# Modulation product of an adaptive-norm layer: where its vector steps ride, and how its partial sums cross the partitions

## The reference, cut to what matters

```
c_act = silu(c)
mod = c_act @ w_ada + b_ada                     # 1024 x 6144
shift1, scale1, gate1, shift2, scale2, gate2 = split(mod, 6)
h = rms_norm(x, g_pre_mix) * (1 + scale1) + shift1
y = token_mixer(h, ...)                         # GLU, convolution, attention
x = x + gate1 * rms_norm(y, g_post_mix)
h = rms_norm(x, g_pre_mlp) * (1 + scale2) + shift2
y = square(relu(h @ w_mlp_in)) @ w_mlp_out
x = x + gate2 * rms_norm(y, g_post_mlp)
```

## Time and profile before

| | before |
|---|---|
| median of 3 runs | 1105.59 us (1102.8 to 1105.71) |
| the profiled execution | span 1101.8 us from the first to the last instruction; no time of its own is listed beside it |
| TensorE busy | 1076.2 us, 98% |
| VectorE busy | 814.3 us, 74% |
| ScalarE busy | 550.6 us, 50% |
| POOL busy | 49.7 us, 5% |
| moved by DMA | 205.85 MB |

### The profile page before, as it was taken

The page is one execution under the profiler, slowest core; times in us unless marked ns, Lnnn a source line. Parts: engine busy times, 40 slices in busy tenths (PEclk is TensorE's granted clock), DMA queues, the critical chain, the costliest instruction groups (busy, mean ns, idle before and its releaser), DMA issues.

```text
span 1101.8 us, 18585 instructions
## 1 busy us (share of the span) xinstructions
PE 1076.2 (98%) x7422; PEld 906.7 (82%) x7422; DVE 814.3 (74%) x1163; ACT 550.6 (50%) x682; POOL 49.7 (5%) x58
## 2 busy tenths in 40 slices
PE   9999999999999998999999999999999999999997
PEld 8888888888778777777788888898967888999996
DVE  5665544538689788788999987999997877555554
ACT  6545543436455545553343556375545665444443
POOL 0000000000000441001111000000000000000000
PEclk9999999999999999999999999999999999999999
DMA  9695556453344321969999954374621553565632
GB/s 317 224 273 190 171 172 227 153 192 115 115 153 139 76 54 54 315 213 326 362 330 357 311 188 153 105 230 132 221 78 39 191 191 115 178 204 163 217 117 112
DMA packets 138413, 205.85 MB, mean 187 GB/s; under 512 B 19608, under 2 KB 95661, under 8 KB 138350
## 3 DMA queue, kind: packets, MB, share of 16 engines
q1 hardware_dynamic: 128996, 177.94, 49.6%
q0 software_dynamic: 6560, 25.19, 6.6%
q10 hardware_dynamic: 2794, 1.84, 0.5%
HBM read 202.33 MB, written 1.57 MB: 185 GB/s over the span
## 4 chain that ended last, share of the span: by engine, by line
PE 79%; DVE 13%; DMA 3%; ACT 3%; issue 2%; SPq 0%; POOL 0%; DVEq 0%; ACTq 0%
PE ps L769 22%; PE ps L771 22%; PE ps L770 22%; DVE wl L2594 3%; PE ps L1243 2%; PE ps L995 2%; DMA raw<-in_ffn_w_up 1%; PE ps L1683 1%; DVE wide L3386 1%; DVE wide L2708 1%; PE ps L846 1%; ACT wh L1806 1%; PE ps L1511 1%; PE ps L1180 1%; PE ps L1665 1%
## 5 line engine op out<-in xcount | busy, mean ns | idle before, releaser
L2594 DVE TENSOR_TENSOR wl<-raw,wh 128x2048 fp32r<-128x2048 f32 (+2 forms) x154 | 345.1, 2246 | 84.8 <-ACT wh L1806 84.5
L769 PE MATMUL ps<-wh,xh 128*128 128x512 f32 (+3 forms) x856 | 335.3, 392 | 4.2 <-DVE wl L2594 1.8
L771 PE MATMUL ps<-wl,xh 128*128 128x512 f32 (+3 forms) x856 | 328.3, 384 | 0.0
L770 PE MATMUL ps<-wh,xl 128*128 128x512 f32 (+3 forms) x856 | 327.8, 383 | 0.0
L1806 ACT ACTIVATE wh<-raw 128x2048 fp32r<-128x2048 f32 (+2 forms) x154 | 286.9, 1878 | 50.0 <-PE ps L771 28.4
L769 PEld LDWEIGHTS ps<-wh,xh 128*128 128x128 f32 x856 | 160.9, 188 | 38.5 <-DVE wl L2594 3.8
L771 PEld LDWEIGHTS ps<-wl,xh 128*128 128x128 f32 x856 | 160.8, 188 | 31.6
L770 PEld LDWEIGHTS ps<-wh,xl 128*128 128x128 f32 x856 | 161.0, 188 | 30.2 <-issue 1.0
L769 PE MATMUL ps<-wh,gh 128*128 128x512 f32 x288 | 112.8, 392 | 1.9 <-issue 1.1
L770 PE MATMUL ps<-wh,gl 128*128 128x512 f32 x288 | 112.3, 390 | 0.0
L771 PE MATMUL ps<-wl,gh 128*128 128x512 f32 x288 | 112.1, 389 | 0.0
(11 more groups left out here) (452 smaller groups left out, 1286.0 us busy)
## 6 DMA issues: line engine op xcount, KB each, us to landing
wide<-in_w_ada POOLq DMA_DIRECT2D x24, 1024.0 KB, 9.9
raw<-in_ffn_w_gate SPq DMA_DIRECT2D x44, 512.0 KB, 4.6
raw<-in_ffn_w_up SPq DMA_DIRECT2D x44, 512.0 KB, 5.6
raw<-in_ffn_w_down SPq DMA_DIRECT2D x22, 1024.0 KB, 5.2
raw<-in_w_mlp_in SPq DMA_DIRECT2D x16, 1024.0 KB, 7.1
raw<-in_w_mlp_out SPq DMA_DIRECT2D x16, 1024.0 KB, 4.9
raw<-in_w_in SPq DMA_DIRECT2D x16, 512.0 KB, 4.9
raw<-in_w_in SPq DMA_DIRECT2D x8, 1024.0 KB, 5.3
```

Source lines behind the costliest of these rows:

```text
L769: pe.matmul(o, lh, rh, start=start, stop=False)
L770: pe.matmul(o, ll, rh, start=False, stop=False)
L771: return pe.matmul(o, lh, rl, start=False, stop=stop)
L2594: v.tensor_tensor(wl[:, s, 0:width], raw[:, s, 0:width], f32(wh[:, s, 0:width]), ALU.subtract).then_inc(lo_ready[s], 1)
```

## The change

The product is cut into 24 loads of 128 partitions x 4 rows x 512 columns (still 1 MB each), used by steps of 512 columns, 96 in all. The first 16 loads (shift and scale, 64 steps) ride in the first FFN, from its second chunk to its tenth; the last 8 (gates, 32 steps) in the first eight chunks of the second. There are three buffers instead of four; load j goes into buffer j mod 3 once the step that last read it is counted, and the steps take the loads in pairs. The first three loads are issued after the `ya` transposes. ScalarE fills two of the zero areas after the first chunk of the first FFN, and one ahead of the second.

The sums over partitions leave TensorE. POOL stores the partial sums to DRAM, adds the upper half of the rows onto the lower half by seven accumulating transfers, each waiting for the last, and reads the one row that is left: shift and scale element by element into columns, the gates broadcast to all partitions. VectorE and ScalarE wait for the first store before they write the turned tile over the sums, VectorE for the second before it clears the padding of the convolution's input. `gain_rows` multiplies in place from SBUF. VectorE's loop of the first FFN is written out instead of looped.

```diff
-        ada_raw = [W3(w, KT) for w in (7, 9, 3, 4)]
-        ada_acc = wide[:, 0:6 * D]
+        def ada_raw(j):
+            return W3((7, 2, 3)[j % 3] if j < NADA_EARLY else (7, 9, 3)[j % 3], 4)
...
+            def load_next_ada(j):
+                pool.wait_ge(S("ada_step"), 8 * ((j - 3) // 2) + 7 + (j - 3) % 2)
+                load_ada(j)
+            def partition_sums(md, acc, name):
+                n = acc.shape[1]
+                pool.dma_start(md, acc).then_inc(S(name + "_stored"), 16)
+                pool.wait_ge(S(name + "_stored"), B(name + "_stored") + 16)
+                rows = md.rearrange("p (a n) -> p a n", n=D)
+                for i in range(7):
+                    m = P >> (i + 1)
+                    pool.dma_start(rows[0:m], rows[m:2 * m], accum_op=ALU.add, max_dma_last_dim=4 * D).then_inc(S(name + "_tree"), 16)
+                    pool.wait_ge(S(name + "_tree"), B(name + "_tree") + 16 * (i + 1))
+            pool.wait_ge(S("wst_masked"), B("wst_masked") + 1)
+            pool.wait_ge(S("ya_T"), B("ya_T") + 2)
+            for j in range(3):
+                load_ada(j)
+            pool.wait_ge(S("acc_zero"), B("acc_zero") + 2)
...
+            for j in range(3, NADA_EARLY):
+                load_next_ada(j)
+            pool.wait_ge(S("ada_step"), 4 * NADA_EARLY)
+            partition_sums(ada_md, wide[:, 0:4 * D], "ada")
+            for n in range(2):
+                pool.dma_start(modc[:, 3 * n * KT:(3 * n + 2) * KT], ada_md[0, n * 2 * D:(n + 1) * 2 * D].rearrange("(k p) -> p k", p=P),
+                               allow_slow_non_contiguous=True).then_inc(S("mod_in"), 16)
...
+            pool.wait_ge(S("ada_step"), 4 * NADA)
+            partition_sums(gate_md, wide[:, 0:2 * D], "gate")
+            for n, dst in enumerate((GB1(W), side[:, :])):
+                pool.dma_start(dst, gate_md[0, n * D:(n + 1) * D].partition_broadcast(P)).then_inc(S("gate_in"), 16)
...
-                modulation_columns((0, 1), 0)
+                spin(7, 12)
                 tile_transposes("pre", 0)
-                modulation_columns((3, 4), 1)
                 s0, s1 = arrive(("glu", 0, 0)), plan.at["glu", 0, 1][0]
+                spin(7, 8)
...
-            linear("glu", ..., after={(1, 0): turn_u(0), (1, 1): gate_rows, (2, 0): turn_u(1), (3, 0): turn_u(2)})
+            linear("glu", ..., after={(1, 0): turn_u(0), (2, 0): turn_u(1), (3, 0): turn_u(2)})
...
             def ranks_by_mix(n):
                 if n == 0:
+                    zeros(0)
+                    zeros(1)
...
+            act.wait_ge(S("ada_stored"), B("ada_stored") + 16)
             for t, k in ((0, 1), (1, 0)):
...
             add_down("ffn0", u_, 1, 1)
+            v.wait_ge(S("ada_stored"), B("ada_stored") + 16)
             gained_turn(0, 0)
...
+            modulation(0, 0, sc1, "g_pre_mix_2")
+            modulation(1, 3, sc2, "g_pre_mlp_2")
+            v.wait_ge(S("acc_bias"), B("acc_bias") + 64)
+            ffn_loop("ffn1", u_, RIDE1, before_gl=lambda: split(("glu", 0, 0)))
...
-                        v.tensor_tensor(dst[:, o], ps[:, 4 + 2 * n + b, :], W(6, n * D + b * 512, 512), ALU.mult)
+                        v.tensor_tensor(dst[:, o], dst[:, o], W(6, n * D + b * 512, 512), ALU.mult)
...
+RIDE0 = [(0, 0, 0, 0), (2, 2, 2, 2)] + [(2, 2, 1, 2)] * 8 + [(0, 0, 0, 0)]
+RIDE1 = [(1, 1, 1, 1)] * 8 + [(0, 0, 0, 0)] * 3
```

More of the change, by code:

```diff
@@ L1559, in turn_u @@
                 return turns
-            linear("glu", "pre.xl", 4, c0=1, free=glu_free, after={(1, 0): turn_u(0), (1, 1): gate_rows, (2, 0): turn_u(1), (3, 0): turn_u(2)})
+            linear("glu", "pre.xl", 4, c0=1, free=glu_free, after={(1, 0): turn_u(0), (2, 0): turn_u(1), (3, 0): turn_u(2)})
             for n, nw in ((0, QL), (1, KL + ROPE)):
@@ L2693, in add_linear, with ffn_loop @@
                     v.tensor_tensor(h[:, t, o], h[:, t, o], ps[:, 2 * c + t, :], ALU.add).then_inc(S(name), 1)
-            ada_left = [(j, k, b) for j in range(NADA // 2) for k in range(KT) for b in range(2)]
+            ada_left = [(q, k, b) for q in range(NADA // 2) for k in range(4) for b in range(2)]
             def ada(count):
-                for _ in range(min(count, len(ada_left))):
-                    j, k, b = ada_left.pop(0)
-                    buf, n = 2 * (j % 2) + b, 16 * j + 2 * k + b
+                for _ in range(count):
+                    q, k, b = ada_left.pop(0)
+                    j, n = 2 * q + b, 8 * q + 2 * k + b
+                    block, half = ADA_PLACE(j)
                     if k == 0:
[L2704 to L2707, removed]
-                    v.scalar_tensor_tensor(out=o, in0=ada_raw[buf][:, k, :], scalar=ccol[:, k:k + 1], in1=o,
+                        v.wait_ge(ada_loaded[j % 3], 16 * (j // 3 + 1))
+                    if n == 0:
+                        v.wait_ge(S("c_act"), B("c_act") + 1)
+                        v.wait_ge(S("acc_bias"), B("acc_bias") + 32)
+                    elif n >= 2:
+                        v.wait_ge(S("ada_step"), n - 1)
+                    o = wide[:, (block % 8) * 512:(block % 8) * 512 + 512]
+                    v.scalar_tensor_tensor(out=o, in0=ada_raw(j)[:, k, :], scalar=ccol[:, 4 * half + k:4 * half + k + 1], in1=o,
                                            op0=ALU.mult, op1=ALU.add).then_inc(S("ada_step"), 1)
-            def ffn_loop(f, uses, ride=(0, 0, 0, 0), before_gl=None):
+            def ffn_loop(f, uses, rides, before_gl=None):
                 def body(i, last):
+                    ride = rides[i]
                     split_lo(0, uses[0] + i + 1)
-                    if not (isinstance(i, int) and i == 0):
+                    if i:
                         v.wait_ge(S(f + ".mT"), B(f + ".mT") + i)
@@ L2739, in body @@
                         ada(ride[3])
-                body(0, False)
-                if any(ride):
-                    for i in range(1, NFFN - 1):
-                        body(i, False)
-                else:
-                    with v.Fori(1, NFFN - 1) as i:
-                        body(i, False)
-                body(NFFN - 1, True)
+                for i in range(NFFN):
+                    body(i, i == NFFN - 1)
             def mlp_loop():
@@ L2871, in _ @@
             v.wait_ge(S("ffn0.rs"), B("ffn0.rs") + 1)
-            ffn_loop("ffn0", plan.at["ffn0"][0], before_gl=lambda: split(("k", 0, 0)))
+            ffn_loop("ffn0", plan.at["ffn0"][0], RIDE0, before_gl=lambda: split(("k", 0, 0)))
             u_ = plan.at["ffn0"][0]
@@ L3347, in _ @@
             normed("pre", 0)
-            modulation(0, 0, sc1, "g_pre_mix_2")
+            v.wait_ge(S("modc"), B("modc") + 2)
             modulated("pre", 0, 0, sc1, modc)
```

80 lines of the change are left out of this document (30 added, 50 removed).

## The result

The changed kernel takes 1107.51 us (median of 8 runs, 1105.08 to 1110.27), the kernel before 1102.8 beside it (8 runs, 1100.09 to 1105.71): ratio 1.0041, interval [1.003, 1.0053]. It is slower by some 4.7 us where the forecast was 1.0 less than before; 1107.5 lies in the range given, on the other side of the kernel before. The profiled execution has a span of 1105.2 us and took 1107.02.

What follows compares the result with a forecast made beforehand. TensorE was taken to bound the kernel, with four fifths of the span in the last-ending chain. Gains of 5.9 us less losses of 4.9 took 1105.6 to 1104.6 us; whole range 1100.0 to 1112.5.

Steps and rivals of the forecast that it cites:

- gain 1: Second FFN: fewer modulation steps and less traffic per chunk remove the early stall; 3.4 us won, ends 0 and 3.4.
- gain 2: Second FFN into the GLU: shorter idle products replace ones products, so the first GLU product starts sooner; 1.8 us, high 2.7.
- gain 3: Gate products leave TensorE (3.43 us), but VectorE hardly waits past 690 us; 0.7 us won, ends 0 and 3.4.
- loss 1: First FFN, first chunk: ScalarE's two zero fills take 3.71 us against 2.1 of slack; 1.6 us lost.
- loss 2: First FFN: POOL's first 3 MB may delay the second chunk's weight block; 1.2 us lost, 0 to 5.5.
- loss 3: First FFN, later chunks: ride steps may wait for loads in three buffers used in pairs; 1.0 us lost, 4.6 at median landing.
- loss 4: End of first FFN: chunk 9's two ride steps stand before the last split and gating; 1.1 us lost.
- store, accumulating steps: After the first FFN: waiting for the sums' store costs 0, high 6.7; accumulating transfers hide before POOL's bonus products, 0.
- (b): Rival: modulation loads and weights fight for DMA engines in the first FFN; loss 2 5.5, loss 3 4.6; 1112.5 us, chance 0.24.
- (a): Rival: first FFN swallows its loads, loss 2 and loss 3 nothing, gate products yield 2; 1101.1 us, chance 0.28.
- (c): Rival: ones products before the GLU were hidden anyway, gain 2 and gain 3 are nothing; 1107.1 us, chance 0.10.
- (d): Rival: accumulating steps cost as much as the slowest load, 133 us against 97, delaying the recurrence; 1141 us, chance 0.04.

Runs made afterwards that it cites:

- weights-first run: Changed kernel with SP's 2 MB of vector and low-rank loads moved behind the second chunk's weights and first down block, POOL's loads unmoved; ratio to the kernel before 0.9992.
- run with idle products: Changed kernel with 14 and 9 idle TensorE products ahead of the second and third chunks' first blocks in the first FFN; ratio to the kernel before 1.0016.
- run with later loads: Changed kernel with POOL's first three modulation loads issued when the first FFN's norm is done, not after the ya transposes; ratio to the kernel before 0.9992.
- four buffers: Changed kernel with loads after the norm, zero fills inside the norm, and a fourth load buffer filled at once; ratio to the kernel before 0.9993.
- the rides moved: Kernel with four buffers, with the last two ride steps of the chunk before the end moved to earlier chunks; ratio to the kernel before 0.998.

## Why the prediction was wrong

| term of the sum | forecast | shown |
|---|---|---|
| gain 1, second FFN | 3.4 | 3.38 |
| gain 2, into the GLU | 1.8 | 0.87 at the first gated column |
| gain 3, gate products | 0.7 | 1.5 |
| loss 1, zero fills | 1.6 | 4.25, of it 2.39 pause |
| loss 2, first three loads | 1.2 | 5.77, of it 3.30 pause |
| loss 3, later loads | 1.0 | 0, 1.1 and 1.8 in three profiles |
| loss 4, last ride | 1.1 | 1.14 |
| store, accumulating steps | 0 | 0 |

**The gains held in sum.** Gains 2 and 3 gave 2.93 to the end, for 2.5. Gain 2 was half its size: the operand did not come the 0.5 earlier that the prediction added (14.99 for 14.93), so the product came 1.16 sooner and not 1.8, and the first gated column only 0.87. Gain 3 was twice its size.

**The step that failed is the size of loss 2.** The prediction put the second chunk's block at 3 late if all 3 MB of POOL's go ahead of it and at 0 "if POOL's share is smaller", and took 1.2, "nearer the low end". All 3 MB went ahead. The queues of the DMA engines in 65 to 68 us of the changed kernel, POOL's (software) and SP's (hardware): packets, MB, share of the 16 engines' time:

```profile
q0 software_dynamic: 264, 1.02, 91.0%
q1 hardware_dynamic: 263, 0.07, 10.7%
```

It is the same from 62 to 71: POOL's queue has over 90% of the engines' time, and SP's moves 0.05 to 0.08 MB in 3 us, where before it moved 0.75 to 0.83. "SP's queue is not reordered" and "issued at 68.24" took the issue time for given, but SP's issue instructions are themselves held up here: one lasts 7.71 us, and 1.37 when POOL's loads are elsewhere. The block went out 4.8 later (73.01 for 68.24) and took 12.8 to land for 6.8, 10.8 in all against slack of 7.8 (82.88 less 75.0): 3.0 late, and 3.3 of pause because the norm ahead of it was done 0.36 earlier. The weights-first run shows that it was what stood ahead of the block: with POOL's loads at the same time and SP's vectors behind it, the stall is 0.5. The sign that the prediction named for this, ScalarE waiting for ffn_w_up, is the row that shows it (3.54). Its other sign, 162 to 165 us between first and last hidden copy, could not: the stall lies ahead of the first copy (165.2 were measured).

**A term was missing altogether:** what a pause of TensorE costs beyond itself. The trace of before has only one pause in this FFN, of 0.54, and the clock is 1.00 in all of it, so the sum priced a stall at its own length. (In the recurrence the same trace has half clock: 0.80 and 0.77 in 416 to 420 and 420 to 424 us, from a pause of 2.25 on.) The half clock made 4.5 us of the 10.0 lost in the first two chunks (2.83 and 1.70), and the run with idle products shows it by itself. It was nearly as much as the whole gap between the medians.

**Loss 1** was also misread by one instruction. The slack of 2.1 was counted from the low part of the weight block; TensorE's next block also waits for the gating, which VectorE does behind it (102.02 + 0.87 = 102.9 in the trace of before). So the slack was 104.2 - 102.9 = 1.3 and the pause 3.71 - 1.3 = 2.4, as measured; with the half clock behind it the piece lost 4.25.

**Loss 3** was right in mechanism and near in size: of the three tight ones loads 3 and 7 cost, with covers of 3.6 and 4.4 us where 4.2 was worked out, and load 9 did not; three profiles with the same first FFN (the changed kernel and the two runs that edit only the GLU) lose 0, 1.1 and 1.8. Loss 4 came out as worked out. So did the two costs of nothing: the store landed 4 us before it was needed, and the seven accumulating steps were hidden, though they took 38 us (270.1 to 308.1), less than the lowest end of 45.

**The rivals.** (b) named what happened, POOL's loads and the weights at war in the first FFN, and its point of decision, loads that land later than 8 us: the first three took 11.1 in the median. Its 5.5 for loss 2 is near the 5.77 by luck, since half of that is the clock, and its 4.6 for loss 3 did not come. (a) is what the kernel does once loads, fills and rides are placed, and it is worth more than its 4.5: 0.9941 of 1103.25 is 6.5 us. (c) and (d) are out; that (c)'s 1107.1 is close to the 1107.5 measured is luck, for the gains that it denies came. POOL's three loads landed in 11.1 us while SP's transfers issued around them took up to 17.2. The Trainium skill, "DMA: Bandwidth & Descriptors", Queues, rings and completion order, has the engines take packets from the queues in turn. The trace agrees in packets, 264 of POOL's beside 263 of SP's; in bytes POOL's queue went far ahead, for its packets held some 4 KB and SP's some 0.3 KB.

## What to carry to other kernels

When transfers are moved into a stretch where the DMA engines run full, look at the other queue too, at its issues and at its packets: a queue that is held delays everything behind it, the block that is needed next above all, and putting that block first can be worth as much as taking the bytes away. Count slack up to the last thing that the waiting engine waits for, and add to a pause of TensorE the half clock that may follow (here 2.8 us behind one of 3.84, 1.7 behind one of 2.39); idle products kept the clock here, and products that look like pure cost may be doing just that. A change can be right and its placement wrong: here the same work is 0.4% slower or 0.6% faster by where its loads, fills and last steps stand and by a fourth buffer.

## What was not expected of the hardware

The same pause does not always bring the half clock. A pause of 2.39 us did in the changed kernel and one of 2.37 in the run with later loads did not (19.38 to the next copy, clock 1.00); one of 3.03 did with four buffers (21.65) and one of 2.84 with the rides moved did not (19.83). The difference, some 1.6 us, comes and goes between kernels that are alike up to there. What decides it was not tried.

That 3 MB of large packets on one queue leave the small packets of another hardly any bytes is seen in the changed kernel and with the weights first (90 to 94% for POOL's queue from 62 to 71 us). No run changed the packets' size, so that the size is the reason is argued from the equal counts.
